# Mixer kernel: the 64x64 products of HGRN and RWKV laid over four quarters of the array, and RWKV's inverse kept in one form

## The reference

```python
# A, RWKV-7, one token at a time:
sa = einsum('bhij,bhj->bhi', S, a_t)
S = S * w_t + sa[..., None] * b_t + v_t[..., None] * k_t
y = einsum('bhij,bhj->bhi', S, r_t)
# C, HGRN2, by chunks of 64 tokens:
o_inter = einsum('bhtk,bhkv->bhtv', q_c * exp(b_c), S)
att = einsum('bhtk,bhsk,bhtsk->bhts', q_c, k_c, exp(rel))   # causal
o_intra = einsum('bhts,bhsv->bhtv', att, v_c)
S = exp(b_last)[..., None] * S + einsum('bhsk,bhsv->bhkv', k_c * exp(b_last - b_c), v_c)
```

## Time and profile before

| | |
|---|---|
| median of 3 runs | 1109.26 us (1109.11 to 1111.39) |
| the profiled execution | 1111.76 us, span 1110.0 us, clock 0.982 |
| PE busy | 1047.9 us, 94% of the span |
| DVE, ACT, POOL busy | 564.6, 417.8, 282.6 us |

### The profile page before, as it was taken

One profiled execution on the slowest core, in us unless ns is written; L12 is line 12 of the kernel. 1 busy time (PEld: TensorE's weight loads), 2 busy tenths in 40 slices (PEclk: granted clock), 3 DMA queues, 4 the chain that ended last, 5 costly groups with the idle time before them and its releaser, 6 DMA issues.

```text
span 1110.0 us, 22968 instructions
## 1 busy us (share of the span) xinstructions
PE 1047.9 (94%) x9788; PEld 863.6 (78%) x9788; DVE 564.6 (51%) x765; ACT 417.8 (38%) x721; POOL 282.6 (25%) x259
## 2 busy tenths in 40 slices
PE   7999988899899899999979898999999999999997
PEld 5888867876688698677867777888669888888876
DVE  6317998864446834243495784422133354445124
ACT  7313112123645411376734634464640243223112
POOL 3335640011315200112301100432165630315020
PEclk9999999999999999899999899999999999999999
DMA  7111110000111100021100015756762210102013
GB/s 240 33 44 38 49 47 3 3 22 20 29 29 38 39 4 4 2 71 44 39 21 21 2 37 155 232 163 194 228 190 77 70 45 1 46 32 67 10 57 114
DMA packets 78871, 71.04 MB, mean 64 GB/s; under 512 B 4081, under 2 KB 62641, under 8 KB 78770
## 3 DMA queue, kind: packets, MB, share of 16 engines
q1 hardware_dynamic: 78770, 69.57, 20.7%
HBM read 56.97 MB, written 12.58 MB: 63 GB/s over the span
## 4 chain that ended last, share of the span: by engine, by line
PE 72%; DVE 18%; ACT 5%; issue 2%; DMA 1%; POOL 1%; SPq 0%; DVEq 0%; ACTq 0%; POOLq 0%
PE units L985 9%; PE bank L1256 8%; PE bank L1257 7%; PE bank L1258 7%; PE bank L934 7%; DVE yT L1565 6%; PE bank L936 6%; PE bank L935 6%; PE bank L974 5%; DVE A L1562 4%; ACT B L1279 2%; PE bank L969 2%; PE duo L1201 2%; PE duo L872 2%; PE bank L1229 1%
## 5 line engine op out<-in xcount | busy, mean ns | idle before, releaser
L934 PE MATMUL bank<-act_hi,whi 128*128 128x512 f32 x464 | 191.2, 412 | 0.0
L936 PE MATMUL bank<-act_hi,wlo 128*128 128x512 f32 x464 | 182.4, 393 | 0.0
L935 PE MATMUL bank<-act_lo,whi 128*128 128x512 f32 x464 | 182.2, 393 | 0.0
L985 PE MATMUL units<-A 64*64 64x64 f32 x4608 | 152.8, 222 | 26.0 <-DVE A L1728 13.3
L857 POOL TENSOR_SCALAR whi<-wraw 128x512 fp32r<-128x512 f32 x66 | 56.3, 853 | 468.3 <-PE bank L936 389.1
L985 PEld LDWEIGHTS units<-A 64*64 64x64 f32 x4608 | 145.4, 138 | 38.5 <-issue 19.1
L1879 DVE TENSOR_TENSOR_SCAN B<-B 128x512 f32<-128x512 f32 (+3 forms) x48 | 48.5, 1009 | 120.6 <-ACT B L1279 119.7
L934 PEld LDWEIGHTS bank<-act_hi,whi 128*128 128x128 f32 x464 | 87.7, 189 | 22.8 <-issue 4.1
L858 POOL TENSOR_TENSOR wlo<-wraw,whi 128x512 fp32r<-128x512 f32 x66 | 102.9, 1558 | 5.5
L1256 PE MATMUL bank<-vhi,act_hi 128*128 128x512 f32 (+1 forms) x288 | 103.3, 359 | 0.8 <-POOL vlo L844 0.7
L1257 PE MATMUL bank<-vlo,act_hi 128*128 128x512 f32 (+1 forms) x288 | 102.5, 356 | 0.0
(11 more groups left out here) (208 smaller groups left out, 1732.4 us busy)
## 6 DMA issues: line engine op xcount, KB each, us to landing
wraw<-in_w_in SPq DMA_DIRECT2D x62, 256.0 KB, 2.9
A<-in_x SPq DMA_DIRECT2D x8, 512.0 KB, 7.3
x<-in_x SPq DMA_DIRECT2D x8, 512.0 KB, 7.9
moved<-in_wv SPq DMA_DIRECT2D x16, 256.0 KB, 4.8
keys_dram<-moved SPq DMA_DIRECT2D x16, 256.0 KB, 2.2
vals_dram<-moved SPq DMA_DIRECT2D x16, 256.0 KB, 4.3
vraw<-in_w_out SPq DMA_DIRECT2D x16, 256.0 KB, 2.9
vraw<-keys_dram SPq DMA_DIRECT2D x16, 256.0 KB, 2.6
```

What stands on the lines that cost most here:

```text
L934: mm(bank, wh, act_hi[:, k, cols], start=k == 0, stop=False)
L935: mm(bank, wh, act_lo[:, k, cols], start=False, stop=False)
L936: ins = mm(bank, wl, act_hi[:, k, cols], start=False, stop=k == KT - 1)
L985: ins = mm(bank[r, c * CH:(c + 1) * CH], a(r, col), b(r, col), start=n == 0, stop=n == len(terms) - 1)
```

## The change

- **Token rows by chunk parity.** A row with tokens on its partitions now has even chunks on partitions 0 to 63 and odd ones on 64 to 127; its two halves of columns are the two heads. `to_tokens` multiplies rows over channels (input partitions by head) into such rows (output partitions by parity), `all_to_channels` goes back. With both, four consecutive products are in four quarters of the array. Both open the two banks at once and do a full block.
- **The inverse.** `invt` makes dTT alone, from a transposed rTT that `tmat` makes anew each level: 8 transposes of 128x128, read by one ACT and one DVE copy 128x512. The dT products (4 levels x 2 halves), their masked copies, and the start of rT in `minit` go.
- **Turns** of b, hv, hk (ACT) and k (DVE) are read by one copy 128x512 for a half instead of two and two of 64x256. The turn of a is as before.
- **Stages are no longer halves**: after each block two readers take a bank each (`xk`, `w1`, `w2`, `tokv`, `tmat`: one ACT, one DVE; `mk3`, `hh`, `gt`, `qq`, `invt`, `hlev`: DVE takes both; `invp`: ACT takes both).
- **What stays on two quarters**: `minit`, the state terms of `yy` and of `hout`, `cs`. These terms now follow a wait (`y_tokens`, `hout_tokens`) until the token terms are out.
- `TILE_ORDER` and `MERGE` are new. Between `invp` of level 1 and `mk3` there are 1 piece and 9 convolution steps for p = 0 (before 4 and 18), and 5 pieces and 1 stick-breaking turn for p = 1 (before none); between `mk3` and `cs` 8 pieces and 10 steps (before 3 and 6), and 6 pieces (before 2); in the 14 `cs` of p = 0, 9 pieces and 6 steps (before 13 and 2).

```diff
+            def to_tokens(key, lhsT, rhs):
+                bank = [rw.pe_open(pe, key + (n,)) for n in range(2)]
+                for c in range(NC):
+                    for hd in range(2):
+                        to, _ = token_at(c, hd)
+                        ins = mm(bank[hd][to, c // 2 * CH:(c // 2 + 1) * CH], lhsT(c, hd), rhs(c, hd), start=True, stop=True)
+                        if c == NC - 1:
+                            rw.pe_post(ins, key + (hd,))
+            def all_to_channels(key, *terms):
+                bank = [rw.pe_open(pe, key + (n,)) for n in range(2)]
+                for j in range(NC // 2):
+                    for n, (a, b) in enumerate(terms):
+                        for c in (2 * j, 2 * j + 1):
+                            for hd in range(2):
+                                ins = to_channels(bank, c, hd, a, b, start=n == 0, stop=n == len(terms) - 1)
+                            if j == NC // 2 - 1 and n == len(terms) - 1:
+                                rw.pe_post(ins, key + (c % 2,))
...
-            def invt(p, l, h):
-                rw.wait_read(pe, ("P1", p, l, h))
-                bank, post = unit(rw, ("dTT", p, l, h))
-                pairs(bank, h, of(rT), of(rP1), post)
-                if l < 5:
-                    bank, post = unit(rw, ("dT", p, l, h))
-                    pairs(bank, h, of(rP1), of(rT), post)
+            def tmat(p, l):
+                inverse_read(p, l)
+                for q in range(2):
+                    bank = rw.pe_open(pe, ("tmat", p, l, q))
+                    for c in range(4):
+                        at = (4 * q + c) * P
+                        ins = tr(bank[:, c * P:(c + 1) * P], A[:, rTT, at:at + P], ident)
+                    rw.pe_post(ins, ("tmat", p, l, q))
+            def invt(p, l):
+                all_read(rw, ("invp", p, l))
+                all_read(rw, ("tmat", p, l))
+                all_to_channels(("invt", p, l), (token(rT), token(rP1)))
...
+            def hlev(p, l):
+                pe.wait_ge(sem("hz_ready"), 2 * (6 * p + l) + 2)
+                to_tokens(("hlev", p, l), chan(hlev_buf(p, l)), chan(hlev_buf(p, l)))
```

More of the change, by code:

```diff
@@ L146, in mixer_chains @@
         step(rec, ("rwb", i))
-        halves(rec, ("tok", "v", i), lambda h: [proj("rw", i, "v")])
+        step(rec, ("tokv", i), proj("rw", i, "v"))
         step(rec, ("bon", i))
@@ L152, in mixer_chains @@
         for l in range(1, 6):
-            halves(rec, ("invp", i, l), lambda h: [("invt", i, l - 1, h) if l > 1 else ("minit", i, h)])
-            halves(rec, ("invt", i, l), lambda h: [("invp", i, l, h)])
+            step(rec, ("invp", i, l))
+            step(rec, ("tmat", i, l))
+            step(rec, ("invt", i, l))
         for w in ("ak", "rb", "rk"):
[L156 to L163, removed]
+            step(rec, ("mk3", w, i))
+        halves(rec, ("tok", "a", i), lambda h: [("mk3", "rb", i)])
+        for w in ("xk", "w2", "w1", "hh", "gt", "qq"):
+            step(rec, (w, i))
         for c in range(1, NC - 1):
@@ L515, in program @@
             elif name == "tok":
-                rw.plan((name,) + a, reads=1 if a[0] == "v" else 4)
-            elif name in ("hdiag", "hlev", "hkv", "hout"):
-                rw.plan((name,) + a)
+                rw.plan((name,) + a, reads=4 if a[0] == "a" else 1)
             elif name == "minit":
-                rw.plan(("L",) + a, reads=2)
+                rw.plan(("L",) + a)
                 rw.plan(("M",) + a)
[L522 to L529, removed]
+            elif name in ("hdiag", "hlev", "hkv", "hout", "tokv", "invp", "tmat", "invt", "mk3", "xk", "w2", "w1", "hh", "gt",
+                          "qq", "yy"):
+                for n in range(2):
+                    rw.plan((name,) + a + (n,))
+            elif name == "cs":
                 rw.plan((name,) + a)
@@ L990, in unit, with all_read, to_channels, chan @@
                 return ring.pe_open(pe, key), lambda ins: ring.pe_post(ins, key)
+            def all_read(ring, *keys):
+                for key in keys:
+                    for n in range(2):
+                        ring.wait_read(pe, key + (n,))
+            def to_tokens(key, lhsT, rhs):
[6 more added lines that the diff above has]
+                            rw.pe_post(ins, key + (hd,))
+            def to_channels(bank, c, hd, lhsT, rhs, first=0, start=True, stop=True):
+                to, _ = chan_at(c, hd)
+                j = c // 2 - first
+                return mm(bank[c % 2][to, j * CH:(j + 1) * CH], lhsT(c, hd), rhs(c, hd), start=start, stop=stop,
+                          skip_group_check=not (start and stop))
+            def all_to_channels(key, *terms):
[7 more added lines that the diff above has]
+                                rw.pe_post(ins, key + (c % 2,))
+            def chan(i):
+                def at(c, hd):
+                    r, col = chan_at(c, hd)
+                    return A[r, i, col]
+                return at
+            def token(i):
+                def at(c, hd):
+                    r, col = token_at(c, hd)
+                    return A[r, i, col]
+                return at
             def of(i):
@@ new lines, in hkv, with hout @@
+            def hkv(p):
+                for h in range(2):
+                    rw.wait_read(pe, ("tok", "hk", p, h))
+                all_to_channels(("hkv", p), (token(hKt), token(hVt)))
+            def hout(p):
+                for n in range(2):
+                    rw.wait_read(pe, ("hkv", p, n))
+                bank = [rw.pe_open(pe, ("hout", p, n)) for n in range(2)]
+                for c in range(NC):
+                    for hd in range(2):
+                        ins = to_channels(bank, c, hd, token(hVt), token(hatt[p]), start=c < 2, stop=False)
+                        if c == NC - 1:
+                            ins.then_inc(sem("hout_tokens"), 1)
+                pe.wait_ge(sem("hout_tokens"), 2 * p + 2)
+                for c in range(NC):
+                    for hd in range(2):
+                        r, col = chan_at(c, hd)
+                        ins = mm(bank[c % 2][r, c // 2 * CH:(c // 2 + 1) * CH], A[r, hz[p], col], A[r, hq[p], col],
+                                 start=False, stop=True, skip_group_check=True)
+                    if c >= NC - 2:
+                        rw.pe_post(ins, ("hout", p, c % 2))
@@ L1263, in _ @@
             run({"xT": xT, "mT": mT, "part": part, "piece": piece, "lora": lora_, "kkn": kkn, "bon": bon, "tok": tok,
-                 "minit": minit, "invp": invp, "invt": invt, "mk3": mk3, "xk": xk, "w2": w2, "w1": w1, "hh": hh, "gt": gt,
+                 "tokv": tokv, "minit": minit, "invp": invp, "tmat": tmat, "invt": invt, "mk3": mk3, "xk": xk, "w2": w2, "w1": w1, "hh": hh, "gt": gt,
                  "qq": qq, "cs": cs, "yy": yy, "var": var, "cmean": cmean, "cvar": cvar, "hdiag": hdiag, "hlev": hlev, "hkv": hkv, "hout": hout,
@@ L1422, in w2, with invp, tmat, xk @@
-            def w2(p, h):
-                copy_out(rw, ("w2", p, h), A[:, rW2, hs(h)])
+                copied(("L", p, h), A[:, rL, hs(h)])
+            def invp(p, l):
+                for n in range(2):
+                    copied(("invp", p, l, n), level_half(A[:, rP1, hs(n)], l, 1), lambda b: level_half(b, l, 1))
+            def tmat(p, l):
+                key = ("tmat", p, l, 0)
+                rw.rd_done(act, nc.scalar.copy(*by_tokens(rw.rd_open(act, key), A[:, rT, :], 0)), key)
+            def xk(p):
+                copied(("xk", p, 0), every_other(A[:, rX, :], 0), cm)
@@ L1546, in _ @@
                  "proj": proj,
[L1547 to L1548 removed]
+                 "xwt": xwt, "lora": lora_, "rwa": rwa, "kkn": kkn, "tok": tok, "tokv": tokv, "minit": minit,
+                 "invp": invp, "tmat": tmat, "xk": xk, "w2": w2, "w1": w1, "yy": yy,
                  "var": var, "csq": csq, "cvar": cvar, "cfin": cfin, "hgate": hgate, "hlev": hlev,
```

361 lines of the change are left out of this document (188 added, 173 removed), and 33 rows, old and new, of tables (MERGE, TILE_ORDER).

## The result

The changed kernel takes **1142.49 us** (median of 4 runs, 1139.27 to 1143.01), the kernel before 1109.18 beside it: a ratio of 1.028 (1.026 to 1.031), slower by 33 us by the medians and 31 by the ratio. The forecast was 1093.5, the range 1078 to 1120.

The account below looks back on a forecast made before the run. PE, busy 94% of the span, was taken as the bound, DVE in HGRN's levels. Gains of 6 + 4.6 + 1.2 (`yy`) + 8, less 4 for the clock, made 15.8 us less: 1093.5 us, range 1078 to 1120.

Parts of the forecast that it names:

- q: Time of a whole block's products on four quarters: 1.02 us, the middle between 0.93 and 1.15.
- The rival in which four quarters give nothing: Four quarters gain nothing or little over two: a block stays at 1.87 us, the kernel at 1132 us; chance 0.13.
- A level of the inverse, 2q + 3.97, 6.01 us: RWKV's inverse: each level takes two blocks plus 3.97 us of hand-overs and copies; five levels 30.6 us.
- the rival of the clock: The clock falls in RWKV's inverse too, block 1.71 us: 1112 us, between 1104 and 1118; chance 0.12.
- `mk3` to `cs`, 25.3 us: RWKV's chain from the masked products to the state steps: 10q + 15.1 us in whole blocks.
- `tokv` to `invp`, q + 10.8: RWKV's chain from the values' turn to the inverse's first product: one block plus 10.8 us.
- Second part, gain 4.6: RWKV's second part, net of pieces and stick-breaking: 62.7 us before, 58.1 after, 4.6 us less.
- First part, gain 6: RWKV's first part, net of pieces: 70.1 us before, 62.2 after, less 2 given back by convolution steps: 6 us gained.
- HGRN, gain 8: HGRN's two parts: 4 us gained in each, of the 8 to 10 us PE idled there.
- The clock, -4: Slow stretches in HGRN's levels and just behind were to take 4 us of the gain back.
- PE's busy time -60, idle +45: Sign for the profile after: PE busy about 60 us less and idle 45 us more, busy 90% of the span.
- The new order at nothing: The new order of tiles was costed at nothing.

Follow-up runs that it names:

- e8: The changed kernel with extra products that nobody reads in RWKV's pauses alone, none from HGRN's first gate on (247 products): 1126.91 us, ratio 1.016.
- e12: e11 with extra products that nobody reads in the pauses of RWKV's first part: 1111.43 us, ratio 0.999.
- e2: The changed kernel with its stages in the order of the kernel before, each whole block where its first half stood: 1155.92 us, ratio 1.042.
- e9: The kernel before, in its own order, with the change in RWKV's first part alone: 1126.71 us, ratio 1.015.
- e11: e9 with the changed kernel's order from the values' turn to the last state step of the first part: 1116.36 us, ratio 1.004.
- e13: The changed kernel in its own order with HGRN and RWKV's second part back in halves on two quarters: 1129.97 us, ratio 1.019.
- e4: The changed kernel with 19 more projection pieces moved into the pauses of RWKV's second part: 1134.04 us, ratio 1.022.
- e7: e4 with 17 more pieces put between HGRN's first levels: 1145.94 us, ratio 1.031.

## Why the prediction was wrong

*q, the block on four quarters.* Right: forecast 1.02 us between 0.93 and 1.15, measured 0.94. The rival in which four quarters give nothing (chance 0.13) is refuted. The floor of 25 ns between starts that the Trainium skill gives (TensorE: Matmul & The Clock Gate, Back-to-back issue gap) would make a block's 64 records take 1.6 us; the measured 0.015 us a record decides against it for four 64x64 tiles (a product is two records; inside a block three starts follow each other by 0.006 to 0.009 us, the fourth by 0.036). One reading was off without weight in the sum: on two quarters a quarter streams one record in 0.058 us, not two.

*A level of the inverse, 2q + 3.97, 6.01 us.* Nearly right: 6.28 measured where the clock is up. PE idles in the three places named, 1.72, 0.61 and 1.16 us; the 1.72 is above the 1.3 that the rival of the clock was dismissed with. Five levels came to 34.7 us, five pieces within, against 30.6; 33.1 in e8.

*`mk3` to `cs`, 25.3 us.* Right at the full clock (26.6 in e8, six pieces within), 32.8 as it ran.

*`tokv` to `invp`, q + 10.8.* Wrong, the first term mis-sized: 17.3 us, one piece within, against 11.8. In DVE's queue the scan of stick-breaking and its product stand between the values' turn and their copy, and PE waits 3.01 us for it:

```profile
387.79 2.60 DVE L1992 TENSOR_TENSOR_SCAN B<-B 128x512 f32<-128x512 f32 x2 [1.81 <-ACT B L1346]
...
390.43 1.23 DVE L1647 TENSOR_TENSOR B<-duo,B 128x1024 f32<-128x1024 f32 x1
391.69 0.69 DVE L1816 COPY A<-units 128x512 f32<-128x512 f32 x1
...
392.52 2.05 PE L1067 MATMUL units<-A,fcst 128*128 128x512 f32 x2 [3.01 <-DVE A L1816]
```

I had added up the chain's own readers. The same stretch took 15.4 us in the kernel before (375.65 to 391.02), so its trace could have told.

*Second part, gain 4.6.* Measured: net 62.2 to 73.0, a loss of 10.8. In e8, which kept the clock from the inverse on, net 66.9: so 6 of it is the clock. The 66.9 is 8.8 over the forecast of 58.1, and 5.5 of that is the term above. *First part, gain 6:* net 69.0 to 70.0; 66.0 in e8.

*HGRN, gain 8.* Wrong: net 0.8 and 1.3 us worse. The levels were to take 4.1 us, with room for q up to 1.3; at the slow clock the block is 1.67 (1.99 less the last record's share), beyond that bound, and DVE waits 0.51 us for it. The levels of the first part took 4.0 to 5.3 us. I took the levels as DVE's, priced the slow clock at 4 us in all, and did not put it back into the level.

*The clock, -4.* **The step that failed.** The term for the slow clock was 4 us, for HGRN alone; by the account it cost 42 us more than before. That the clock falls in RWKV too was a rival, with the right size of the slow block (1.71 forecast, 1.67 measured), a chance of 0.12 and a worst of 1118. Its case was too mild: I looked for single gaps as long as HGRN's (2.9 us) and found none over 1.3 in the inverse. But in the earlier trace rows PE had been busy 7.4 of 9.5 us where the clock stayed up, and in a level it now works 3.4 of 6.3. The rival also looked in the wrong place: of the 34 us at 0.50 in RWKV's second part, 6.8 are in the inverse and 23.9 behind it, in `mk3` to `hh`. The first part has 35 us at 0.50, HGRN 44, and the pieces behind RWKV's parts 27. Slow stretches grew from 39 to 158 us, and also the pieces that stand in them ran slow, 13 us of the 42.

*PE's busy time -60, idle +45.* Work at the full clock -68, idle +57; busy as recorded only -25.9, since the slow clock adds to it. The sum of my terms for work and pauses (some 15 us less) came out as 11 less (-68 + 57); the clock turned it into 31 more. That is an account and not a proof that a full clock would give 1100: e8 and e12, which kept it by extra work, gave 13 and 5 us back by the ratios.

*The new order at nothing.* Open in part. With whole blocks everywhere it is worth 13 us (e2). With whole blocks in the first part alone it pays there and costs elsewhere: e9, e11 and e13 have the same blocks, e9 the old order, e11 the new one in the first part's stretch, e13 the new one throughout. By the ratios e11 is 1.0% faster than e9 and e13 1.4% slower than e11. So the new order costs outside that stretch, where the blocks are halves, and by e9 and e11 the places of the taps and pieces in one stretch carry 11 us. Of the 2.8%, undoing HGRN gave 0.3, undoing the second part 0.6, and the first part costs 0.4 in a mended order; the remaining 1.4% is the order with what it does to clock and pauses elsewhere, and I did not divide it further. Half blocks on four quarters, which would keep the alternation, were not tried: a whole block uses both banks of the ring, so halves would need four.

## What to carry to other kernels

A stage that is bound by PE and runs without a pause has two things that a faster form takes away: the cover over the other engines' copies, and the clock. Before halving PE's work in a chain, work out how long PE will be idle in the new period, and price the whole period, its neighbours' pieces too, at both clock levels. Here PE had worked 3.4 of 6.28 us in the level after which the clock fell to 0.50. Filling the pauses helps only with work that no other stretch needs as cover (e4) and whose reader is not the engine that the chain waits for (e7).

## What the runs showed of the hardware

The records of 64x64 products laid over four quarters start 0.015 us apart on average, on two quarters 0.029 (a product is two records). At the granted clock of 0.50 the four-quarter block's starts are 0.026 apart, so it does not quite double. Tiles of the same rows and different columns overlap, loads included: the 64 loads of a block take 0.13 us each and cover 1.05 us together. A 128x128 product of 128 columns from `ident_r` took 0.128 us on average (145.2 us for 1133). In the changed kernel the granted clock was 0.50 for 23.9 us on end in RWKV's second part with PE busy 16.2 us of it, and in HGRN's levels for 23.7 us with 12.5 busy; in the inverse of e8's second part it was 1.00 for 33.1 us with 28.6 busy.
